# One decoder layer and a second mixing block on one core: the norms' roots from PSUM, tanh in place of sigmoid, the second residual and its gate heads rebuilt

## What is computed

```
# first block
u     = rms_norm(x, ln_mix_pre)
mixed = concat(hgrn2_mixer(u @ w_in ...), dilated_attention(u @ w_in ...)) @ w_out      # 8 + 8 heads of 128
h     = x + rms_norm(mixed, ln_mix_post)
y     = conv_gated_mlp(rms_norm(h, ln_ffn_pre))                                          # 2048 -> 2 x 5632 -> 2048
h     = h + rms_norm(y, ln_ffn_post)                                                     # the second residual
h     = h + (p @ w_pe) * sigmoid(h @ w_pg)                                               # per-layer input behind a gate
# second block
proj  = rms_norm(h, norm_g) @ w_in_2
u     = silu(layernorm(causal_conv31(cv_a * sigmoid(cv_b)))) @ w_conv_pw * silu(cv_gate)
y_fox = fox_attention(...) * silu(fox_gate)                                              # 8 heads
y_mem = memory_attention(..., rms_norm(mem) @ w_mem_kv) * silu(mem_gate)                 # 4 heads
out   = rms_norm(h + concat(u, y_fox, y_mem) @ w_out_2, final_g)
# rms_norm(x, w) = x * rsqrt(mean(x * x) + EPS) * w ;  silu(x) = x * sigmoid(x)
```

## Time and profile before

| | before |
|---|---|
| runs | 1852.43, 1853.12, 1854.91 us (median 1853.12) |
| the profiled execution | 1853.38 us, its span 1851.6 us |
| PE busy | 1800.9 us, 97% of the span |
| DVE, ACT, POOL busy | 1282.6 us (69%), 960.8 us (52%), 653.2 us (35%) |
| HBM | 323.85 MB read, 176 GB/s over the span |
| mean granted TensorE clock | 0.992 of full |

### The profile page before, as it was taken

One profiled execution on the slowest core, in us unless ns is written; L12 is line 12 of the kernel. 1 busy time (PEld: TensorE's weight loads), 2 busy tenths in 40 slices (PEclk: granted clock), 3 DMA queues, 4 the chain that ended last, 5 costly groups with the idle time before them and its releaser, 6 DMA issues.

```text
span 1851.6 us, 29943 instructions
## 1 busy us (share of the span) xinstructions
PE 1800.9 (97%) x10306; PEld 1569.7 (85%) x10306; DVE 1282.6 (69%) x1584; ACT 960.8 (52%) x1276; POOL 653.2 (35%) x639
## 2 busy tenths in 40 slices
PE   9999999999989999999999999999899999999996
PEld 7888888888878888888888888888788888878885
DVE  6676666665578777777777544446787778888754
ACT  5564555445456555555555433335555666764532
POOL 3723444444743333211111322223452255450033
PEclk9999999999999999999999999999899999999998
DMA  8434444445554555555555455555455444443452
GB/s 316 146 132 159 160 161 164 172 160 205 187 206 179 193 187 181 184 192 190 181 183 195 163 187 187 187 187 191 145 193 195 144 175 159 159 159 137 161 188 105
DMA packets 50284, 326.56 MB, mean 176 GB/s; under 512 B 5696, under 2 KB 6336, under 8 KB 17600
## 3 DMA queue, kind: packets, MB, share of 16 engines
q1 hardware_dynamic: 49664, 323.86, 49.4%
q10 hardware_dynamic: 576, 2.11, 0.3%
HBM read 323.85 MB, written 2.10 MB: 176 GB/s over the span
## 4 chain that ended last, share of the span: by engine, by line
PE 83%; DVE 7%; issue 4%; ACT 3%; DMA 1%; SPq 1%; POOL 0%; DVEq 0%; ACTq 0%; POOLq 0%
PE ps L1759 52%; PE ps L1760 27%; DVE wlo L926 2%; PE ps_lev L1834 2%; ACT whi L438 1%; DMA stage<-in_w_a 1%; DVE fge L949 1%; DVE fs L1477 1%; PE ps_t L1788 0%; ACT usq L814 0%; DVE fge L1481 0%; DVE tmp L932 0%; DVE y L1219 0%; ACT small L445 0%; PE ps_t L2065 0%
## 5 line engine op out<-in xcount | busy, mean ns | idle before, releaser
L1759 PE MATMUL ps<-act_a,whi 128*128 128x512 f32 x3072 | 1092.3, 397 | 10.7 <-DVE tmp L932 8.4
L926 DVE TENSOR_TENSOR wlo<-stage,whi 128x2048 fp32r<-128x2048 f32 (+1 forms) x316 | 701.5, 2221 | 248.8 <-ACT whi L438 244.9
L1760 PE MATMUL ps<-act_a,wlo 128*128 128x256 f32 x3072 | 869.3, 283 | 0.0
L1759 PEld LDWEIGHTS ps<-act_a,whi 128*128 128x128 f32 x3072 | 578.5, 188 | 144.9 <-DVE tmp L932 7.7
L438 ACT ACTIVATE whi<-stage 128x2048 fp32r<-128x2048 f32 (+1 forms) x316 | 568.9, 1801 | 122.4 <-DMA stage<-in_w_down 105.5
L1760 PEld LDWEIGHTS ps<-act_a,wlo 128*128 128x128 f32 x3072 | 579.0, 188 | 0.3
L1759 PE MATMUL ps<-big,whi 128*128 128x512 f32 x1600 | 566.0, 396 | 9.1 <-DVE big L1333 7.3
L1760 PE MATMUL ps<-big,wlo 128*128 128x256 f32 x1600 | 453.4, 283 | 0.0
L1759 PEld LDWEIGHTS ps<-big,whi 128*128 128x128 f32 x1600 | 301.5, 188 | 80.1 <-DVE big L1333 5.6
L445 ACT ACTIVATE small<-ps 128x256 f32<-128x256 f32 x248 | 94.8, 382 | 520.4 <-PE ps L1760 520.3
L1760 PEld LDWEIGHTS ps<-big,wlo 128*128 128x128 f32 x1600 | 301.9, 189 | 0.1
(11 more groups left out here) (338 smaller groups left out, 1400.9 us busy)
## 6 DMA issues: line engine op xcount, KB each, us to landing
stage<-in_w_a SPq DMA_DIRECT2D x166, 1024.0 KB, 4.8
stage<-in_w_b SPq DMA_DIRECT2D x87, 1024.0 KB, 4.8
stage<-in_w_down SPq DMA_DIRECT2D x64, 704.0 KB, 4.0
stage<-in_w_a SPq DMA_DIRECT2D x8, 256.0 KB, 9.7
mem_raw<-in_memT SPq DMA_DIRECT2D x1, 2048.0 KB, 9.2
mem_again<-in_memT SPq DMA_DIRECT2D x1, 2048.0 KB, 9.1
out<-o_out SPq DMA_DIRECT2D x4, 512.0 KB, 2.7
x_in<-in_xT ACTq DMA_DIRECT2D x3, 512.0 KB, 8.8
```

Source lines behind the costliest of these rows:

```text
L926: dve.tensor_tensor(wlo[:, slot, part], stage[:, slot, part], whi[:, slot, part].bitcast(F32), ALU.subtract).then_inc(w_lo, 1)
L1759: pe.matmul(dst, whi[:, slot, c * P:(c + 1) * P], act, start=start, stop=False)
L1760: return pe.matmul(dst[:, T:2 * T], wlo[:, slot, c * P:(c + 1) * P], act[:, 0:T], start=False, stop=stop)
```

## The change

1. **Norms.** `mean_square` is gone. ACT takes the sum straight from PSUM: Ln with scale 1/2048 and a bias tile `eps`, then Exp (`norm` with its PSUM operand; all norms but the convolution's). `ln_ahead` loads the Ln table ahead of time in six places.
2. **Gates.** sigmoid(x) becomes (1 + tanh(x/2))/2, where Tanh shares the table of Exp. The factor one half is taken into `scaled`, `fox_gated`, `memory_gated` or the pointwise product; DVE multiplies (tanh + 1) by x in one instruction (SCALAR_TENSOR_TENSOR). For the fox and memory heads one such instruction (`twice_gated`) stands in place of the three of `logistic`. The gate of `w_pg` keeps its Sigmoid.
3. **Second residual.** The last tile of y is squared on ACT, into `y_sq`, and summed by a second matmul. DVE does all multiplications and additions of the residual, with the split of one quarter between the steps of the next; POOL does none.
4. **`p @ w_pe`.** Two output tiles share a bank, seven banks are used in turn, and ACT copies a pair (128x512) at once.
5. **Gate heads.** The first two gate blocks run quarter by quarter, side by side.
6. **Order.** The transposes of the last fox head come halfway through the block behind them; those of the last memory head, and its output, one conv-gate block later.

```diff
+            def norm(t, name, sums):
+                act.wait_ge(*event(name + "_summed"))
+                link(act.activation(t, sums, ACT.Ln, scale=1.0 / D, bias=eps[:, 0:1]))
+                act.activation(t, t, ACT.Exp, scale=-0.5).then_inc(event(name + "_norm")[0], 1)
...
-                act.activation(fge[:, :], fgx[:, :], ACT.Exp, scale=-1.0).then_inc(s("fg_exp"), 1)
+                act.activation(fge[:, :], fgx[:, :], ACT.Tanh, scale=0.5).then_inc(s("fg_tanh"), 1)
...
-            def logistic(e, exp_done, n):
-                dve.wait_ge(s(exp_done), n)
-                link(dve.tensor_scalar(e, e, LARGE, 1.0, ALU.min, ALU.add))
-                link(dve.reciprocal(e, e))
...
-                link(dve.tensor_tensor(fge[:, :], fge[:, :], fgx[:, :], ALU.mult))
+            def twice_gated(e, x, tanh_done, n):
+                dve.wait_ge(s(tanh_done), n)
+                link(dve.scalar_tensor_tensor(out=e, in0=e, scalar=1.0, in1=x, op0=ALU.add, op1=ALU.mult))
...
-            keep(range(3))
-            norm(rstd[:, :], "y")
-            keep(range(3, 7))
+            norm(rstd[:, :], "y", ps_a)
             hi(G_PE, 0, 0, 3)
-            keep(range(7, 11))
+            keep(range(4))
             split_h2(0)
-            keep(range(11, 13))
+            keep(range(4, 7))
             split_h2(1)
-            keep(range(13, 16))
+            keep(range(7, 8))
             split_h2(2)
             split_h2(3)
...
-            for j in range(4):
-                whole(G_PG, 0, 0, j, U_PG + j, j % 2, xs_h,
-                      ready=None if j else lambda c: pe.wait_ge(s("xs_h"), c * QUARTERS // KT + 1))
+            for c in range(QUARTERS):
+                for j in range(2):
+                    if c == 0:
+                        pe.wait_ge(s("pe_kept"), len(pair_banks) - 1 + j)
+                        await_block(G_PG, 0, 0, j, U_PG + j)
+                    ins = cells((G_PG + j) % NS, j, xs_h, range(KT)[quarter(c)], opens=c == 0, closes=c == QUARTERS - 1,
+                                ready=None if j else lambda c: pe.wait_ge(s("xs_h"), c * QUARTERS // KT + 1))
+                    if c == QUARTERS - 1:
+                        ins.then_inc(w_used, 1)
+            for j in range(2, 4):
+                whole(G_PG, 0, 0, j, U_PG + j, j % 2, xs_h)
...
-                memory_turned(n - 1) if n else fox_turned(HEADS - 1)
-                whole(G_MEM, 0, 0, 2 * n + 1, u + 1, 1, act_a)
+                if n:
+                    memory_turned(n - 1)
+                    whole(G_MEM, 0, 0, 2 * n + 1, u + 1, 1, act_a)
+                else:
+                    await_block(G_MEM, 0, 0, 1, u + 1)
+                    cells((G_MEM + 1) % NS, 1, act_a, range(KT // 2), closes=False)
+                    fox_turned(HEADS - 1)
+                    cells((G_MEM + 1) % NS, 1, act_a, range(KT // 2, KT), opens=False).then_inc(w_used, 1)
```

More of the change, by code:

```diff
@@ L495, in recurrence_out, with tanh @@
                 act.activation(xs_mix[:, bass.ds(n, 1), 0:T], osb[:, :].unsqueeze(1), ACT.Copy).then_inc(s("o_hi"), 1)
[L497 removed]
+            def tanh(e, x, lin, done, i, scale=1.0):
                 wait(act, lin, i + 1)
[L499 removed]
+                act.activation(e[:, :], x[:, :], ACT.Tanh, scale=scale).then_inc(s(done), 1)
             def turned(dst, ready, done, i):
@@ L537, in second_head @@
                 hi(start, 1, 8, 3)
-                sigmoid(ef, hfx, "hf_lin", "hf_sig", 1)
+                tanh(ef, hfx, "hf_lin", "hf_tanh", 1, scale=0.5)
                 attention_turned(0)
@@ L541, in second_head @@
                 hi(start, 1, 8, 4)
-                sigmoid(eq, hqx, "hq_lin", "hq_sig", 1)
+                tanh(eq, hqx, "hq_lin", "hq_tanh", 1)
                 attention_out(0)
@@ L573, in mixers_head @@
                 hi(start, i, 8, 3)
-                sigmoid(ef, hfx, "hf_lin", "hf_sig", i)
+                tanh(ef, hfx, "hf_lin", "hf_tanh", i, scale=0.5)
                 attention_turned(before)
@@ L577, in mixers_head @@
                 hi(start, i, 8, 4)
-                sigmoid(eq, hqx, "hq_lin", "hq_sig", i)
+                tanh(eq, hqx, "hq_lin", "hq_tanh", i)
                 attention_out(before)
@@ L596, in mixers_head @@
                     hi(start, i, 8, 9)
-                sigmoid(eg, hgx, "hg_lin", "hg_sig", i)
+                tanh(eg, hgx, "hg_lin", "hg_tanh", i)
                 if memory:
@@ L766, in _ @@
             split_h3(KT - 1)
-            act.activation(dummy[:, 1:2], ones[:, 0:1], ACT.Ln)
+            ln_ahead()
             for n in range(GROUPS):
@@ L1656, in _ @@
                              lambda i: pool.wait_ge(out_free, U_OUT + i + 3), "mixed", "ln_mix_post")
-            def residual(t, name):
-                by_norm = rstd[:, :].unsqueeze(1).to_broadcast([P, KT // QUARTERS, T])
-                last = quarter(QUARTERS - 1)
-                pool.wait_ge(*step(name + "_gain", KT))
-                link(pool.tensor_tensor(t[:, last, :], t[:, last, :], by_norm, ALU.mult))
-                for c in range(1, QUARTERS):
-                    if c < QUARTERS - 1:
-                        pool.wait_ge(*step(name + "_scaled", c + 1))
-                    pool.tensor_tensor(h[:, quarter(c), :], h[:, quarter(c), :], t[:, quarter(c), :], ALU.add)\
-                        .then_inc(step("h2_ready", 0)[0], 1)
             pool.wait_ge(s("xs_u"), KT)
```

215 lines of the change are left out of this document (118 added, 97 removed).

## The result

| | before | after |
|---|---|---|
| median of 4 runs | 1853.72 us | 1810.14 us (1807.80 to 1810.65) |
| ratio to before | | 0.9763, 95% interval 0.9746 to 0.9779 |
| the profiled execution, its span | 1853.38, 1851.6 us | 1810.18, 1808.4 us |
| PE busy | 1800.9 us | 1776.9 us |

The account below looks back on a forecast made before the run. The prediction took PE, busy 97% of the span, as the bound, with gains only from its waits and slow clock; terms summing to 25.2 us off 1853.4, adjusted to the runs' median, gave 1828.0 us, range 1821.5 to 1836.

Parts of the forecast that it names:

- The change does not shorten a product: All PE products: each stays at 0.351 us, so the change pays only where PE stands still or runs slowly.
- A: First norm: the sum goes straight to ACT, the add comes earlier and PE's wait goes, 1.2 us.
- D: Starts of six fox heads: one DVE instruction replaces three, PE's wait of 1.04 us each goes, 6.3 us.
- C: Second residual and gate blocks: earlier residual chain, third gate block starts at 1307.4 us, worth 9.7 us.
- The rule on DVE and POOL: Second residual: shared SBUF interfaces contend; with POOL waiting the weight split takes 2.28 us, not 4.47.
- E: Last fox head: eight products cover the 2.36 us wait, and the clock's fall behind it goes, 3.8 us.
- F: Last memory head: its output, one block later, no longer waits for a copy on ACT, 1.5 us.
- G: End of the kernel: mean_square leaves the last chain, 0.4 us.
- B: First residual: DVE's chain starts 1.7 us early; the norm behind it gains 0.6 us.
- The rival with a fall at the rebuilt residual: Second residual: remaining waits bring the clock down, a loss of 3.1 us, total 1831.1 us; chance 0.16.
- The slower rival: DVE in the heads: (tanh + 1) * x meets POOL, delaying PE 1.45 us in 20 heads, 1857 us; chance 0.03.

Follow-up runs that it names:

- e2: The change with eps in a third column of dummy, so that act_a and big lie where they lay before: 1826.74 us, ratio 0.9855.
- e10: e2 with the first two gate blocks one behind the other instead of side by side: 1831.95 us.
- e4: The kernel before with the whole map, weights and activations alike, 32 bytes higher: 1854.39 us, ratio 1.0000.
- e3: The kernel before with an unused tile of 64 bytes ahead of act_a and big: 1863.95 us, ratio 1.0052.
- e1: The kernel before with an unused tile of 32 bytes where the change has eps: 1838.24 us, ratio 0.992.
- e13: The kernel before with 32 unused bytes between wlo and whi, activations further from wlo alone: 1858.22 us, ratio 1.0021.
- e14: The kernel before with 32 unused bytes between wlo and whi and dummy moved behind big, activations nearer to whi alone: 1838.05 us, ratio 0.9917.
- e9: e2 with the old gate, Exp and three instructions on DVE, in the fox heads alone: 1834.47 us.
- e7: e2 with the activations 160 bytes above their place of before, a single run: 1807.45 us.
- e11: e2 with the activations 160 bytes above their place of before, timed in four runs: 1809.86 us.

## Why the prediction was wrong

- **The step that failed is the first one: "The change does not shorten a product."** It does, by 4.44 ns in each of 4704, 20.9 us of products of which 16.6 reach the end. I read the pace from a row, took it as a property of the instruction, and didn't look at where the tiles lie, though the new tile `eps` ahead of `act_a` is in the diff. No rival had it. The Trainium skill (TensorE: Matmul & The Clock Gate, "Back-to-back issue gap") gives N/2.4 + 2.5 ns as the gap of an isolated matmul of N columns at the higher clock, and says that in a stream of weight loads and matmuls both set the spacing. By the formula a product of 512 and 256 columns would take 325 ns, an estimate from that page. The runs here show 346.7 to 353.3 ns for the same columns and the same weight loads, so the measurement decides, and a rule of columns alone doesn't give the pace in this kernel.
- **With the pace held (e2), the sum holds:** 27.0 us against 25.2, and 1826.7 us against 1828.0, inside the range. The sum is in part closer than its terms: A and D were short by 2.4 us together, and 1.1 went back to a longer stretch at half clock. C came out to 0.1 us, by the intermediate times too. The rule on DVE and POOL that was weighed there holds as well: the split took 2.29 us, with POOL waiting.
- **D was short by 1.5 us.** It counted the waits alone, 1.04 us per head. A head became shorter by 1.30 us. E, F and G hold to 0.2 us.
- **A was short by 0.9.** The second head's wait for `sm` at 61.8 us, which I had left as it was, shrank from 1.42 to 1.0 us, and the first norm gave 0.4 more than the wait.
- **B was right in sum, and its start to 0.1:** the multiplication in e2 starts 1.7 us earlier than before, once the 1.0 us gained till then is taken off. 
- **In C one wait was misread,** here and in the section on the change. I let the second gate block wait 1.4 us for the eighth pair. The code waits for six and seven pairs, `len(pair_banks) - 1 + j`, which are there in time; the trace has no such wait. It cost nothing, since the last low half sets the end.
- **The clock.** The rival with a fall at the rebuilt residual didn't come true: 1.00 there in e2 and in the change. e10 shows that it was near, since behind a wait of 1.83 us it fell. The evidence that I set against this rival was one execution's: behind the same wait at the first residual, 2.06 us, e4 has 3.4 us at half clock where the kernel before and e3 have none, and e1, e13 and e14 (2.02 to 2.13 us) have them too. Nor was 2.2 us a bound. E has such a part as well: the fall behind the last fox head that it counts at 1.4 us is there in before, e4, e13 and e14, but not in e1 and e3, which have the same wait there (2.3 to 2.6 us in all six). Behind the wait at 96 us it stayed at half for 10.24 us in e2 and the change, where before had 6.8: the -1.1 us of the table. That isn't the change's doing: the kernel before with its map moved (e4) shows 10.24 too, and e9, a version of the change, 6.8.
- **The slower rival** had the right mechanism and no effect on the time. Where the new instruction meets POOL, it takes 1.51 us, as in the last fox head of e2 and of the change; in the other fox heads and the memory heads it doesn't meet it and takes 0.41 to 0.42.

## What to carry to other kernels

In this kernel a matmul's pace was a reading of one memory map, not a constant: an idle tile of 32 bytes made the old kernel 0.8% faster, one of 64 bytes 0.5% slower, as much as a rebuilt stage is worth. When tiles are added or taken away, compare the time per matmul in a stretch without waits first, and try a few idle bytes ahead of the activations; hold the pace equal before you credit or blame a change of order. And adding up every instruction ahead of the awaited one gave the worth of five of the seven steps to 0.2 us, and missed the other two by 0.9 and 1.5; it counted the waits, and not what else a stage loses with them. Take the clock from more than one execution: a fall that one trace shows behind a wait, another lacks.

## What the hardware showed that was not expected

- The dependence itself: 0.3467, 0.3500, 0.3511, 0.3517 and 0.3533 us for one product of 512 and 256 columns at a granted clock of 1.00, by steps of 32 bytes in how the activations, with the tiles moved along with them, and the two weight buffers lie to each other. Its rule is open.
- The stretch at half clock behind one and the same wait of 3.8 to 4.1 us in the second head was 3.4, 6.8 or 10.24 us long in different executions. Two executions of one kernel, e7 and e11, had 3.4 and 6.8.
- In three traces, which of DVE and POOL is slowed went with which started first. POOL's last addition ahead of the norm took 2.87 us where DVE's weight split started with it (change, e1) and 0.74 where it started 0.08 us ahead of the split, which then took 2.80 instead of 2.29 (e2). No run moved the two on purpose.
- An instruction on DVE that reads two tiles of 128x256 takes 0.41 to 0.43 us alone and 1.35 to 1.51 us beside POOL, the product of two and the new instruction alike.
